# One ring of four slots for landed weights and their low parts, in a float32 kernel of two transformer blocks

## The reference

```
x += 0.5 * (silu(h @ w_gate) * (h @ w_up)) @ w_down            # d_ff 2816, four times
p  = h @ w_in                                                   # 7 x 1024 columns and some, twice
x += (sigmoid(gate_a) * (y_a @ w_proj_a) + sigmoid(gate_b) * (y_b @ w_proj_b)) @ w_out
mod = silu(c) @ ada_w + ada_b                                   # 1024 -> 6144, twice
q, k, v = h @ w_qkv ; y = attention(q, k, v) @ w_o
x += g * conv_ffn(h)                                            # 1024 -> 5632 -> 1024
```

## Time and profile before

| | us |
|---|---|
| median of 3 runs | 3530.27 |
| the runs | 3529.68, 3530.27, 3537.05 |
| profiled execution | 3531.23 |
| its span, first to last instruction | 3529.3 |
| PE busy | 3066.8 (87%) |
| DVE busy | 2077.2 (59%) |
| ACT busy | 1485.8 (42%) |
| transfers of the stream: share of the 16 DMA engines | 33.4% |

### The profile page before, as it was taken

How to read it: one execution, slowest core, us unless ns; L and a number is a source line. 1 busy time by engine, 2 the same in 40 slices (tenths; PEclk the granted TensorE clock), 3 DMA queues, 4 the chain that set the end, 5 groups by cost and what they waited for, 6 DMA issues and landing times.

```text
span 3529.3 us, 41271 instructions
## 1 busy us (share of the span) xinstructions
PE 3066.8 (87%) x15258; PEld 2504.7 (71%) x15258; DVE 2077.2 (59%) x2589; ACT 1485.8 (42%) x1870; POOL 99.9 (3%) x149
## 2 busy tenths in 40 slices
PE   7995999899999959998999886976598899789797
PEld 6874788777888737887778675755477677567676
DVE  4557666555455586666555676455457476445465
ACT  4433111534344431015344454365456365347463
POOL 0001000000000100000000000000000000001000
PEclk9997999999999979999999998998899899899899
DMA  5554000444545640004445793421134335341243
GB/s 190 190 205 173 1 1 19 155 163 171 192 177 187 213 157 1 1 19 161 158 176 190 290 341 136 154 90 54 55 119 165 139 150 188 113 167 46 108 166 119
DMA packets 76079, 485.44 MB, mean 138 GB/s; under 512 B 9342, under 2 KB 13516, under 8 KB 21792
## 3 DMA queue, kind: packets, MB, share of 16 engines
q1 hardware_dynamic: 60608, 440.43, 33.4%
q0 software_dynamic: 10720, 38.84, 3.2%
q10 hardware_dynamic: 4608, 4.20, 0.5%
HBM read 474.74 MB, written 2.13 MB: 135 GB/s over the span
## 4 chain that ended last, share of the span: by engine, by line
PE 64%; DVE 11%; ACT 7%; issue 5%; DMA 5%; DVEq 5%; ACTq 2%; POOL 0%; POOLq 0%; SPq 0%; PEldq 0%
PE ACC L371 53%; PE M L371 5%; DVE w_lo L1280 5%; DMA raw<-wstream 3%; PE TP L371 3%; ACT w_hi L868 2%; PE TP L447 2%; ACTq L1197 1%; DMA BC<-vecs 1%; DVEq L1864 1%; DVEq L1869 1%; ACT PR L1128 1%; ACT CV L1206 1%; DVE HV L1874 0%; DVE ST L1789 0%
## 5 line engine op out<-in xcount | busy, mean ns | idle before, releaser
L1280 DVE TENSOR_TENSOR w_lo<-raw,w_hi 128x2048 fp32r<-128x2048 f32 x375 | 847.8, 2290 | 532.5 <-ACT w_hi L868 514.7
L371 PE MATMUL ACC<-w_hi,HA_hi 128*128 128x512 f32 (+1 forms) x2256 | 906.4, 402 | 62.6 <-DVE w_lo L1280 16.2
L868 ACT ACTIVATE w_hi<-raw 128x2048 fp32r<-128x2048 f32 x375 | 707.7, 1917 | 508.4 <-DMA raw<-wstream 279.9
L371 PE MATMUL ACC<-w_lo,HA_hi 128*128 128x512 f32 (+1 forms) x2256 | 894.4, 396 | 0.0
L371 PE MATMUL ACC<-w_hi,HA_lo 128*128 128x512 f32 (+1 forms) x2256 | 892.5, 396 | 0.0
L371 PEld LDWEIGHTS ACC<-w_hi,HA_hi 128*128 128x128 f32 x2256 | 437.3, 194 | 164.2 <-issue 28.7
L371 PEld LDWEIGHTS ACC<-w_hi,HA_lo 128*128 128x128 f32 x2256 | 436.1, 193 | 92.4
L371 PEld LDWEIGHTS ACC<-w_lo,HA_hi 128*128 128x128 f32 x2256 | 436.5, 193 | 86.9
L371 PE MATMUL ACC<-w_hi,FT_hi 128*128 128x512 f32 x616 | 247.0, 401 | 24.3 <-ACTq L1197 18.3
L371 PE MATMUL ACC<-w_lo,FT_hi 128*128 128x512 f32 x616 | 245.1, 398 | 0.0
L371 PE MATMUL ACC<-w_hi,FT_lo 128*128 128x512 f32 x616 | 244.9, 398 | 0.0
(11 more groups left out here) (311 smaller groups left out, 3888.3 us busy)
## 6 DMA issues: line engine op xcount, KB each, us to landing
raw<-wstream SPq DMA_DIRECT2D x375, 1024.0 KB, 4.9
RAWX<-wstream SPq DMA_DIRECT2D x44, 1024.0 KB, 7.0
BC<-vecs POOLq DMA_DIRECT2D x33, 512.0 KB, 6.3
BIAS<-toe ACTq DMA_DIRECT2D x32, 128.0 KB, 2.8
BC<-mod_scr POOLq DMA_DIRECT2D x6, 512.0 KB, 6.4
PREV<-R POOLq DMA_DIRECT2D x4, 448.0 KB, 6.0
PREV<-K POOLq DMA_DIRECT2D x4, 448.0 KB, 5.1
PREV<-V POOLq DMA_DIRECT2D x4, 448.0 KB, 3.5
```

The lines of the kernel that those rows point to most:

```text
L371: return pe.matmul(*a, skip_group_check=True, **k)
L868: act.activation(w_hi[:, s, :], unit, ACT.Copy).then_inc(sem["hi_ready"], 1)
L1280: dve.tensor_tensor(w_lo[:, s, :], unit, w_hi[:, s, :].bitcast(F32), ALU.subtract).then_inc(sem["lo_ready"], 1)
```

## The change

`raw` gets four slots, and `w_lo` is laid over it: the low part of a unit is written in the place where the unit landed. The two arrays `raw` and `w_lo` together take 32 KiB of a partition instead of 48. A slot is now free only when PE is done with the low part in it, so that the transfer of unit u waits for `unit_done` of unit u-4. At the start four transfers are issued at once instead of two. There are four landing semaphores. The two first transfers behind the wide stretch were issued when `lo_ready` had reached units 218 and 219; now there are four of them, each behind `unit_done` of the unit four before it. Transfers of the wide stretch itself wait as before.

```diff
-RAW, SPLIT = 2, 4
+RAW, SPLIT = 4, 4
@@ build
-        raw = sb("raw", [P, RAW, UNIT])
+        ring = place["at"]
+        raw, w_lo = sb("raw", [P, RAW, UNIT]), sb("w_lo", [P, SPLIT, UNIT], F32R, at=ring)
         w_hi = sb("w_hi", [P, SPLIT, UNIT], F32R)
-        w_lo = sb("w_lo", [P, SPLIT, UNIT], F32R)
@@ sync
             with eng.Fori(1, WIDE_FROM // RAW) as i:
                 for s in range(RAW):
-                    eng.wait_ge(sem["lo_ready"], i * RAW + (s + 1 - RAW))
+                    eng.wait_ge(sem["unit_done"], i * RAW + (s + 1 - RAW))
...
             for u in range(WIDE_TO, WIDE_TO + RAW):
-                eng.wait_ge(sem["lo_ready"], WIDE_FROM - RAW + u % RAW + 1)
+                eng.wait_ge(sem["unit_done"], u + 1 - SPLIT)
                 eng.dma_start(raw[:, u % RAW, :], wstream[u]).then_inc(sem[f"land{u % RAW}"], 16)
             with eng.Fori(WIDE_TO // RAW + 1, NUNITS // RAW) as i:
                 for s in range(RAW):
-                    eng.wait_ge(sem["lo_ready"], i * RAW + (s + 1 - RAW))
+                    eng.wait_ge(sem["unit_done"], i * RAW + (s + 1 - RAW))
...
             for u in range(NUNITS // RAW * RAW, NUNITS):
-                eng.wait_ge(sem["lo_ready"], u + 1 - RAW)
+                eng.wait_ge(sem["unit_done"], u + 1 - RAW)
@@ scalar, swiglu (conv_ffn likewise)
-                with e.loop(5, {"land0": 32, "land1": 32, "tp_ready": 2}) as i:
+                with e.loop(5, {"land0": 16, "land1": 16, "land2": 16, "land3": 16, "tp_ready": 2}) as i:
```

More of the change, by code:

```diff
@@ L275, in build @@
         B4 = [TP[0][:, :], TP[1][:, :], M[0][:, :], M[1][:, :]]
-        names = ["land0", "land1", "wide0", "wide1", "wide2", "wide3", "bc0", "bc1", "hi_ready", "lo_ready",
+        names = ["land0", "land1", "land2", "land3", "wide0", "wide1", "wide2", "wide3", "bc0", "bc1", "hi_ready", "lo_ready",
                  "unit_done", "acc_ready", "acc_free0", "acc_free1", "tp_ready", "tp_free0", "tp_free1",
@@ L1218, in conv_ffn @@
                 split(2)
-                with e.loop(5, {"land0": 32, "land1": 32, "tp_ready": 4, "cv_conv": 2, "hv_ready": 2}) as i:
+                with e.loop(5, {"land0": 16, "land1": 16, "land2": 16, "land3": 16, "tp_ready": 4, "cv_conv": 2, "hv_ready": 2}) as i:
                     for b in (1, 2):
```

## The result

The changed kernel takes 3579.72 us (median of four runs, 3575.67 to 3582.61) against 3529.97 us (3525.89 to 3537.05) for the kernel before. The ratio is 1.0138, with a 95% interval of 1.0119 to 1.0157: 1.4% slower. The profiled execution has 3579.84 us and a span of 3577.9 us, against 3531.23 and 3529.3.

The account below looks back on a forecast made before the run. PE is 64% of the chain, transfers 5%, so a later transfer costs only where its unit is late for PE or in-order ACT or DVE. Terms sum to +51.1 us on 3531.23 profiled, giving 3581.3 median, 1.4% more; range 3560 to 3603.

Parts of the forecast that it names:

- start: Start of the kernel: two more units queue beside constants and x, so the first split comes later, +5.0 us.
- three borders: Borders behind a down product: feature rounding stands behind a split waiting for its landing, 5.0 us each, +15.0 us.
- mixers, to the recurrence (tanh, pair ahead of it): Both mixers up to the recurrence: tanh waits go, -11.6 us; the pair ahead costs 1.75 on ACT, 1.4 on DVE.
- mixers, rest (norm, two late places): Later in each mixer: pair ahead of the gated unit's norm costs 1.2 us, two feature roundings behind landings 5.5.
- projections, attention, convolution: Second block: six waits behind later landings cost 9.7 us, five barriers behind attention and convolution 10.6.
- clock: PE's half clock after 5 us stands: two such stands go, three come at the borders, +1.9 us.
- The rule for one unit: Every transfer: unit u's starts when PE ends unit u-4, and it is there 5.0 us after its slot came free.
- Loops: Feed-forward, down-product and convolution loops: later landings are covered by idle time on ACT and DVE, cost nothing.
- rival of the clock: PE's clock falls at each new stand, some nine more at 1.9 us: +17, 3598; 0.08 together with the tanh rival.
- Tanh: Both mixers: unit 42's transfer goes out 6.2 us earlier, so ACT's wait and PE's stand go, -11.6 us.
- half of the border cost is covered: Rival: something unseen covers half the border cost, giving 3556 to 3565 us; chance 0.12.
- faster: Rival: in-order ACT is freed from landing waits at more places than the tanh, 3524 us at a quarter; chance 0.04.

Follow-up runs that it names:

- b_wait: Kernel before, two landing slots and separate low parts, but each transfer also waits for unit_done of unit u-4, SP's program written out: 3584.91 us.
- a_start: Changed kernel, but the third and fourth transfer of the start wait until the first high part is written: 3574.18 us.
- a_border: Changed kernel, but at borders ACT rounds all features before splitting two units, and the pair ahead of the modulation is split behind its barrier: 3566.28 us.
- a_all: Changed kernel with the moves of a_start, a_border, a_mix and a_bar, and the ninth feed-forward low part behind residual and features: 3466.81 us.
- a_mix: Changed kernel, but at the end of the mixer four pairs of splits stand behind the feature rounding that followed them, on ACT and DVE: 3552.86 us.
- a_bar: Changed kernel, but in the second block splits stand behind copies of keys and queries, a stage's last pair behind its barrier and the next features: 3516.96 us.
- b_tanh: Kernel before, but in the mixer ACT does the tanh ahead of the pair of splits behind the third block: 3544.07 us.
- ring6: Low parts over landed units in six slots, transfers waiting for unit_done of u-6, loops written out, two transfers at first, against the kernel before: 3448.21 us.
- b_all: Kernel before, two landing slots, with the same moves as a_all except that of the start: 3478.66 us.
- a_allu: a_all with the seven loops written out: 3421.53 us.
- ring6_all: ring6 with the moves of a_all: 3402.45 us.

## Why the prediction was right, and where it wasn't

The forecast was 3581.3, the chip gave 3579.72. That the total is off by only 1.6 us is in part luck: the second block was put 9.4 us too high, the mixers 7.2 and the modulation 2.7 too low. The terms against the table of stages:

| term | predicted | measured |
|---|---|---|
| start | +5.0 | +4.5 |
| three borders | +15.0 | +15.4 |
| mixers, to the recurrence (tanh, pair ahead of it) | -8.8 | -6.9 |
| mixers, rest (norm, two late places) | +13.4 | +18.7 |
| into the modulation | +4.3 | +3.1 |
| modulation | 0 | +2.7 |
| projections, attention, convolution | +20.3 | +10.9 |
| clock | +1.9 | in the rows above |
| sum | +51.1 | +48.4 |

*The rule for one unit* (slot free + 5.0) held in the loops and down products: units land 4.8 to 5.0 us behind PE's unit, and the landing's median is 4.8. In the mixers, where other queues are busy, single landings took up to 9.1 us. The estimate of 4.4 us a transfer, from the Trainium skill, "DMA: Bandwidth & Descriptors", section "Anatomy of one DMA", would have given 3573; that section states its fit for DMAs issued from GpSimd, which these are not, and the measurement decides for 4.8. *Loops* cost nothing, for the reason given. *Overwriting* at nothing is shown by b_wait. *Start* is shown by a_start.

*Borders*: the sum of 15 was right and its place half wrong; PE stood 2.9, 2.3 and 1.5 us ahead of the first matmul of the next stage, not the 5 us that I had said the profile would show. I wrote that in the down products each unit has 17 us of room. The ninth has not: DVE's residual stands in order behind its low part. Of 5 us at a border 2.1 to 2.4 are lost there (what a_border leaves) and the rest at the split ahead of the rounding. With both moved, in a_all, the first two borders cost nothing.

*Mixers, to the recurrence*: I had taken the second border split as hidden by the shift of the first. In front of a feed-forward part, whose first block is wide, it is. In front of a mixer the first block is narrow, and PE is soon at the features that ACT rounds behind that split. In front of the second mixer:

```profile
1205.79 1.91 ACT L868 ACTIVATE w_hi<-raw 128x2048 fp32r<-128x2048 f32 x1 [4.55 <-DMA raw<-wstream]
...
1209.79 0.50 PE L371 MATMUL ACC<-w_hi,HA_hi 128*128 128x160 f32 x1 [3.71 <-DVE HA_lo L1350]
```

PE stood 1.87 us there before. The first blocks of the mixers lose 1.9 and 3.4 us in this way, half clock behind the stand included. (A whole unit of the mixer takes 5.4 us, 7.3 behind the stand at the tanh, where I had read 5.6 and 7.5; the difference, 1.8, is close to the 1.9 that I used.) At the tanh 8.9 and 9.3 us were gained, where stand and clock had been put at 7.7 and 7.6, and from the last pair on 1.7 and 4.3 were lost, half clock included, instead of 1.4 each.

*Mixers, rest*: the term of the clock failed. It counted one low stretch more; added up over the clock record, the clock stood at 0.50 for 443 us before and 491 us after. In the rest of the first mixer the low time went from 20.5 to 27.3 us, in that of the second from 20.5 to 31.1. Two windows of the second mixer, to be read as the earlier trace rows, in the changed kernel:

```profile
1724.90:1735.10 10.20, 5.74 (x18) 4.75 (x19) 4.97 (x5) 3.60 (x5) 0.00 (x0) 0.50 0.01 2
1776.10:1782.90 6.80, 5.79 (x14) 4.53 (x15) 5.31 (x4) 1.91 (x1) 0.00 (x0) 0.50 0.26 108
```

and the same places before:

```profile
1703.90:1710.70 6.80, 5.87 (x18) 4.88 (x19) 2.91 (x5) 1.19 (x2) 0.00 (x0) 0.50 0.70 287
1748.00:1755.00 7.00, 7.00 (x32) 5.64 (x31) 4.82 (x4) 0.00 (x0) 0.00 (x0) 1.00 0.47 169
```

PE's busy time at the lower clock grew from 232 to 245 us, which is some 6 us of time, not 1.9. The rival of the clock was wrong in its size (17), but not in its kind: stands of 2.8 and 3.6 us ahead of unit 72 and its like had half clock behind them. At this place the two mixers lost 4.4 and 6.5 us, where the term of 2.7 had only the stand; at the other late place, which is one stand with the norm of the gated unit, they lost 2.5 and 3.1 where the two terms had 3.5. In the second mixer ahead of the recurrence the low time was 68.3 us where it had been 61.4, and the gain was 1.6 where the first mixer had 5.3; a_start, a_mix and a_bar, with 65 and 61 us, gained 4.3 to 6.7 there. That the clock makes this difference is argued, not shown, and a_all speaks against a simple rule: it has 68.3 us of low time there and gains 3.3.

*Second block*: the terms were right, but I didn't ask what got shorter. The six waits of the projections grew by 9.0 us (9.7 predicted), the five barriers by 2.1 each (10.6 predicted). Some 9 of these 19.6 us were given back at waits for other things; that nothing covered them was the step that failed here. Behind two barriers what shrank is the wait for the load of the convolution's weights. The waits of PE at the first of them, before:

```profile
2549.57 1.97 PE L447 MATMUL TP<-K__55,X 128*128 128x128 f32 x8 [7.19 <-DVEq L1272]
...
2559.03 1.22 PE L371 MATMUL M<-DIAG,K__55 128*128 128x128 f32 x4 [7.49 <-DVEq L1709]
```

and after:

```profile
2593.44 1.97 PE L447 MATMUL TP<-K__55,X 128*128 128x128 f32 x8 [9.39 <-DVEq L1272]
...
2599.79 1.22 PE L371 MATMUL M<-DIAG,K__55 128*128 128x128 f32 x4 [4.37 <-DVEq L1709]
```

The barrier comes 2.2 us later, and the next wait is 3.1 us shorter (3.7 at the other one, 8.9 to 5.2). The squares behind the diagonal wait for `CW`, which POOL loads behind the barrier. The DMA issues of the stretch (count, KB, us to landing), before and after:

```profile
CW<-convw POOLq DMA_DIRECT2D x1, 88.0 KB, 5.3
```

```profile
CW<-convw POOLq DMA_DIRECT2D x1, 88.0 KB, 2.2
```

Before, two stream transfers of 1 MiB went out just then, at 2547.3 and 2549.5, the load at 2549.8; now the stream's transfers had gone one by one, and the last had landed at 2589.0, before the load went out at 2593.7. So a change that starts transfers later also takes them out of the way of a small load on the path. I had asked only what the later transfer would collide with.

*Tanh*: right for the changed kernel, and wrong as I valued it. b_tanh shows that the stand alone is worth nothing with two landing slots, since their ring, with longer landings in it, then sets the pace of that stage; the changed kernel and ring6, where PE frees the slots, keep the gain. Of the rivals, *half of the border cost is covered* came true in the second block only, and *faster* failed as forecast.

## What to carry to other kernels

Where an engine works in order, a wait that is moved to a later event costs what stands behind it, not what it waits for: list, for each place, the next thing that others need, on every engine that takes part (ACT's split and DVE's low part each had one). Moving prefetch work behind that thing was worth 113 us here (a_all against the changed kernel), more than the change cost, since much of it had been on the path before the change too; but work moved too far back becomes late itself, as PE's waits for low parts show. Before a stall is counted as a gain, ask what else has the same pace; and when transfers move, ask whose small load was in their way.

## What the chip showed that was not expected

Writing out the seven loops of 20 units took 50 us off (b_unroll, against 3531.57 for the kernel before on the same chip), nearly all in the three convolution parts, 15 to 16 us in each, of which some 13.5 in the loop. The four feed-forward loops lost nothing by being loops. In a turn of two blocks of the convolution loop ACT loads its function table twice (30 such loads in the kernel before, 3 written out), and waits 0.3 us where the written-out turn has nothing; DVE, the bound there, begins its pairs of low parts at 2609.91, 2624.04 and 2636.74, 14.1 and 12.7 us apart; written out they are at 2603.91 and 2615.74, 11.8 apart. How much of it is the loads and how much the waits was not separated. The timeline of ACT in a loop of the kernel before:

```profile
2615.79 1.28 ACT L1196 ACT_TABLE_LOAD   x1
...
2623.99 1.28 ACT L1213 ACT_TABLE_LOAD   x1
```

and written out, with no such load:

```profile
2597.75 1.01 ACT L1196 ACTIVATE US<-ACC 128x1024 f32<-128x1024 f32 x1
```

Between a_all and a_allu the same edit took 45.3 us. The modulation varied by 5.5 us between the kernel before and b_tanh, and by 12 between a_all, b_all, a_allu and ring6_all, which have one order there; no run here says why.
